# A two-block transformer kernel: the memory queries of the last attention are scaled one step later, behind the narrow fifth step instead of ahead of it

## What is computed

```python
def mixer_b(h, cos16, sin16, w_in, sinks):          # 16 heads of 64, 4 key heads
    q, k, v, q_mem = split_cols(h @ w_in, B_SPLITS)
    ...                                             # rotary embedding of q and k
    o, _ = banded_window_attention(q, k, v, 127, 64 ** -0.5, sink=sinks)
    return o, q_mem

def memory_cross_attention(q_mem, mem_n, w_mem_kv): # 4 heads of 64, 256 rows of memory
    k, v = split(mem_n @ w_mem_kv)
    p = softmax(q_mem @ k.T * 64 ** -0.5)
    return p @ v

h = rmsnorm(x, g_mix)
mix, q_mem = mixer_b(h, ...)
x = x + concatenate([mix, memory_cross_attention(q_mem, mem_n, w_mem_kv)]) @ w_out
```

## Time and profile before

| | us |
|---|---|
| median of 3 runs | 2058.19 |
| lowest and highest of them | 2058.19, 2059.82 |
| the profiled execution, its time | 2058.34 |
| its span, first to last instruction | 2056.5 |
| busy PE, of the span | 2032.5 |
| busy DVE | 1203.1 |
| busy ACT | 939.2 |
| busy POOL | 1021.9 |

### The profile page before, as it was taken

One profiled execution on the slowest core, in us unless ns is written; L12 is line 12 of the kernel. 1 busy time (PEld: TensorE's weight loads), 2 busy tenths in 40 slices (PEclk: granted clock), 3 DMA queues, 4 the chain that ended last, 5 costly groups with the idle time before them and its releaser, 6 DMA issues.

```text
span 2056.5 us, 30140 instructions
## 1 busy us (share of the span) xinstructions
PE 2032.5 (99%) x11590; PEld 1742.9 (85%) x11590; DVE 1203.1 (59%) x2215; ACT 939.2 (46%) x1525; POOL 1021.9 (50%) x483
## 2 busy tenths in 40 slices
PE   9999999999999999999999999999999999999998
PEld 6888977888898989876878898989887588989997
DVE  4888788674642434477985563646423935545563
ACT  3345545363432334534366642434433956434343
POOL 3434422444675666443713575666343037665663
PEclk9999999999999999999999999999999999999999
DMA  9654322235233333332211433333433033333422
GB/s 372 241 181 147 103 62 62 88 103 178 68 103 103 102 104 103 96 110 67 80 24 55 125 103 102 93 113 94 146 93 75 2 94 106 109 97 103 123 72 92
DMA packets 282550, 220.91 MB, mean 107 GB/s; under 512 B 13520, under 2 KB 266576, under 8 KB 280112
## 3 DMA queue, kind: packets, MB, share of 16 engines
q1 hardware_dynamic: 271712, 195.75, 31.4%
q10 hardware_dynamic: 10704, 23.33, 3.7%
HBM read 213.56 MB, written 2.10 MB: 105 GB/s over the span
## 4 chain that ended last, share of the span: by engine, by line
PE 87%; DVE 7%; issue 2%; ACT 2%; POOL 1%; ACTq 0%; DVEq 0%; POOLq 0%
PE bank L1050 61%; PE bank L1129 12%; PE bank L1349 2%; PE bank L1562 2%; PE bank L1540 2%; DVE arena L3113 1%; PE bank L1497 1%; DVE small L3111 1%; PE bank L1549 1%; PE bank L1650 1%; PE bank L1397 1%; POOL w_split L3301 1%; DVE bank L2580 1%; PE bank L1408 1%; PE bank L1731 1%
## 5 line engine op out<-in xcount | busy, mean ns | idle before, releaser
L1050 PE MATMUL bank<-h_hi,w_split 128*128 128x512 f32 x2832 | 865.1, 382 | 1.9 <-POOL w_split L3301 1.0
L3301 POOL TENSOR_TENSOR w_split<-wslots,w_split 128x2048 fp32r<-128x2048 f32 (+3 forms) x119 | 470.5, 3955 | 631.5 <-ACT w_split L1804 619.9
L1050 PEld LDWEIGHTS bank<-h_hi,w_split 128*128 128x128 f32 x2832 | 534.7, 189 | 93.0 <-issue 16.2
L1050 PE MATMUL bank<-h_lo,w_split 128*128 128x512 f32 x1416 | 537.5, 380 | 0.0
L1804 ACT ACTIVATE w_split<-wslots 128x2048 fp32r<-128x2048 f32 (+2 forms) x114 | 194.1, 1702 | 359.0 <-PE bank L1050 308.8
L1050 PE MATMUL bank<-hid_hi,w_split 128*128 128x512 f32 x1056 | 316.5, 379 | 1.3 <-POOL w_split L3347 0.9
L1050 PEld LDWEIGHTS bank<-h_lo,w_split 128*128 128x128 f32 x1416 | 267.8, 189 | 38.7 <-issue 3.4
L1050 PEld LDWEIGHTS bank<-hid_hi,w_split 128*128 128x128 f32 x1056 | 199.6, 189 | 31.1 <-issue 1.6
L1050 PE MATMUL bank<-hid_lo,w_split 128*128 128x512 f32 x528 | 200.1, 379 | 0.0
L3336 POOL TENSOR_TENSOR entry<-entry_sum,entry 128x512 fp32r<-128x512 f32 x108 | 157.6, 1486 | 74.9 <-ACT entry L2130 74.9
L2580 DVE SCALAR_TENSOR_TENSOR bank<-arena,cols,bank 128x512 f32<-128x512 f32 x240 | 161.3, 751 | 5.4 <-ACT bank L1918 4.9
(11 more groups left out here) (376 smaller groups left out, 3154.5 us busy)
## 6 DMA issues: line engine op xcount, KB each, us to landing
wslots<-in_f_w_up SPq DMA_DIRECT2D x88, 512.0 KB, 5.0
wslots<-in_w_in SPq DMA_DIRECT2D x24, 1024.0 KB, 5.4
wslots<-in_w_ffn_up SPq DMA_DIRECT2D x44, 512.0 KB, 4.8
arena<-in_w_ada ACTq DMA_DIRECT2D x8, 2048.0 KB, 10.5
wslots<-in_a_w_in SPq DMA_DIRECT2D x10, 1024.0 KB, 5.2
arena<-in_w_ada_first SPq DMA_DIRECT2D x8, 1024.0 KB, 18.8
wslots<-in_f_w_down SPq DMA_DIRECT2D x8, 1024.0 KB, 5.1
wslots<-in_f_w_down SPq DMA_DIRECT2D x16, 512.0 KB, 4.1
```

The lines of the kernel that those rows point to most:

```text
L1050: return nc.tensor.matmul(bank[:], w, woven(x), start=start, stop=stop)
L3301: last = nc.gpsimd.tensor_tensor(part[:, 1, cols_of], slot(p, 1, size)[:, 0, cols_of], part[:, 0, cols_of].bitcast(F32), ALU.subtract)
```

## The change

On DVE, the scaling of the memory queries is called at the end of step 4 (`LAG + 1`) instead of step 3 (`LAG`). Nothing else is edited; the table of PE with the wait for the banks stays as it is.

```diff
-            attend(2, {LAG: lambda: scaled_job("b_qmem", 0, [(q_mem[:, m, :], m, P) for m in range(2)])})
+            attend(2, {LAG + 1: lambda: scaled_job("b_qmem", 0, [(q_mem[:, m, :], m, P) for m in range(2)])})
```

## The result

| | us |
|---|---|
| before, median of 20 runs | 2059.17 |
| with the change, median of 20 runs | 2061.77 |
| ratio | 1.0014, 95% interval 1.0008 to 1.0020 |
| profiled execution with the change: time, span | 2061.80, 2060.0 |

By the ratio the change costs 2.9 us (1.6 to 4.1). The prediction said +0.87 us, and its range ended at 2061.2. It also said that this cannot be told from no change at 0.2%. The interval does end at 0.2%, but it leaves out 1.0000, so a loss is shown.

The account below looks back on a forecast made before the run. The prediction took TensorE (PE) to bound the kernel, with 87% of the last chain. A later turn(2) (+1.43 us) and turn(3)'s vanished wait (-0.56) gave +0.87 on 2058.19, so 2059.1 us, range 2057.6 to 2061.2.

Parts of the forecast that it names:

- The sum of the order: PE in the last attention: transposes of turn(2) 1.43 us later, turn(3) regains 0.56 us, together +0.87 us.
- the new wait for the exponentials: On DVE, a reciprocal waits 0.22 us for ACT's exponentials of step 3, which the scaling hid before.
- the later scaling: On DVE, the scaling starts at 1588.73 instead of 1587.30, so PE's turn(2) starts 1.43 us later.
- the vanished wait of turn(3): On PE, the transposes of turn(3) no longer wait for ACT's copy, which ends earlier: -0.56 us.
- rival A: PE's 1.39 us of idle time after 1634 swallows the delay; time 2058.2 us, chance 7%.
- B: Only the loss comes: turn(3) on PE stays as late behind turn(2) as now; 2059.6 us, chance 5%.
- C: PE's bank wait is not what holds turn(2), so only the 0.56 us gain remains; 2057.6 us, chance 2%.
- rival D: PE's clock falls from 2.4 to 1.2 GHz behind its gap ahead of turn(2); 2068.6 us, chance 1%.

Follow-up runs that it names:

- gap_filled_to_fit: The changed kernel with five small products in PE's gap ahead of the wait for the banks; ratio 1.0006 (0.9997 to 1.0015) to the kernel before.
- change_both_filled: The changed kernel with small products in PE's gap ahead of the bank wait and in the first attention's gap; 2059.30 us, ratio 1.0000 to the kernel before.
- scaled_twice: The kernel before, with the two scaling instructions made twice in their old place so that PE's gap grows; ratio 1.0015 (1.0006 to 1.0024).

## Why the prediction was wrong

- **The sum of the order was right.** Forecast +0.87, measured 0.92 with the gap filled. Each term was within 0.05 us: the new wait for the exponentials (0.23 against 0.22), the later scaling, the vanished wait of turn(3), turn(2) at 3.06 behind scores(5) (3.04 forecast).
- **The delay went through to the end, as it said.** PE's later idle times kept their sizes and swallowed nothing (rival A falls). Rivals B and C fell too: in gap_filled_to_fit turn(3) comes 1.57 us behind turn(2), as in the sum, and PE was held by the banks.
- **The step that failed is rival D: the clock behind PE's gap was put at nothing in the sum and at 1% among the rivals.** It was the case that came, and it cost 1.52 us. The prediction put the gap at 2.34 us and had the mechanism and the Trainium skill's rule ("TensorE: Matmul & The Clock Gate", Part 1 on the HAM clock gate, that without activity the clock goes to half rate) beside it. It all but ruled it out by one row, the gap of 2.25 us behind which the clock stayed at 1.00. That row was one execution. The same gap, behind the same instructions, lowered the clock in two of eight traces. The traces agree with the rule: the clock fell behind the gap of 2.36 us, and where that gap was filled (gap_filled_to_fit, change_both_filled) it stayed at 1.00, with everything else as late.
- **D's size was wrong as well.** The prediction let the lower clock last for 10 us of work and priced it at 9.5 us, with nothing between that and no effect at all. The traces show 0.54 over 3.7 us and a price of 1.5 us, to be added to the sum: 0.92 + 1.52 = 2.44. With that term and the median that the kernel before has over 20 runs (2059.17, not the 2058.19 of three), the same working would have given 2061.6; measured were 2061.77.
- **The baseline took 1.0 us.** Three runs, two of them equal, said little about the median. Of the 2.7 us between 2059.1 and 2061.77, the clock is 1.5 and the baseline 1.0; with either one right, the time would have stood inside the range. That does not save the mechanism: against the kernel before, run beside it, the change cost 2.9 us by the ratio and not 0.87. Part of the spread from run to run is, by all appearances, the clock behind the first gap, where two traces pay 0.97 and 1.46 us and six pay nothing.

## What to carry to other kernels

When a wait on a busy TensorE grows, price two things: the wait, and the clock behind it. Where the clock fell behind a gap of 2.2 to 2.4 us, it cost 1.0 to 1.5 us more in the work that followed; the lower price is for slow work that hid a wait which was there anyway. One profiled execution in which a similar gap cost nothing is no proof that the next will not. A few small matmuls in a gap that can't be closed took that price away, and show at the same time how much of a loss is the order's and how much the clock's. Before an operation is moved back in one engine's queue, look for who waits for it by its place in program order: here the wait stood ahead of work that didn't need the banks. Moving the wait alone helped in the trace (+0.35 us) and not by the times (+2.2 us), and PE still had two shorter gaps.

## What the runs showed of the hardware

- The clock of PE did not follow the length of the gap alone. Behind a gap of 2.24 to 2.26 us at the start of the first attention it fell in two of eight profiled executions, behind one of 2.24 us in the last attention in the one profiled (scaled_twice), behind one of 2.36 us there in both profiled ones, and behind a gap in two pieces of 0.62 and 1.11 us, by the mean clocks alone, in about half.
- It did not fall at one fixed point either. With the same gap of 2.36 us it was low from the first transpose on in one execution, and from 1.5 us behind it in another; with a gap of 3.71 us it fell within the gap, and it stayed low until about 1597, 5.5 us behind the gap's end.
- At the lower level a group of four transposes took 1.05 to 1.12 instead of 0.63 us and a pair of 256 wide scores 1.23 instead of 0.70.
